# Hybrid decoder step on one core: query weights of two chunks split between GpSimd's and SP's transfers

## What is computed

```python
q = (xc @ w_q).reshape(PEER_BLOCK, PEER_HEADS, 2, PEER_DK)
s = jnp.einsum('chsk,hsnk->chsn', q, sub_keys).astype(jnp.float32)
sv, si = lax.top_k(s, PEER_TOPK)
cand = sv[:, :, 0, :, None] + sv[:, :, 1, None, :]
...
cs, sel = lax.top_k(cand.reshape(PEER_BLOCK, PEER_HEADS, PEER_TOPK * PEER_TOPK), PEER_TOPK)
...
u = u_tab[eidx]
act = jax.nn.gelu(jnp.einsum('chkd,cd->chk', u, xc).astype(jnp.float32))
w = (g * act).astype(xc.dtype)
return jnp.einsum('chk,chkd->cd', w, v_tab[eidx])
```

## Time and profile before

| | |
|---|---|
| median of 3 runs | 3100.81 us (3096.8 to 3101.7) |
| profiled execution, its own time | 3100.0 us |
| its span | 3097.7 us |
| TensorE matmul busy | 2381.0 us (77%) |
| VectorE busy | 2150.3 us (69%) |
| ScalarE busy | 1003.2 us (32%) |
| GpSimd busy | 1220.6 us (39%) |
| moved | 1229.46 MB, mean 397 GB/s |
| of it by GpSimd's queue | 1082.20 MB, 84.4% of 16 engines' span |

### The profile page before, as it was taken

One profiled execution on the slowest core, in us unless ns is written; L12 is line 12 of the kernel. 1 busy time (PEld: TensorE's weight loads), 2 busy tenths in 40 slices (PEclk: granted clock), 3 DMA queues, 4 the chain that ended last, 5 costly groups with the idle time before them and its releaser, 6 DMA issues.

```text
span 3097.7 us, 40697 instructions
## 1 busy us (share of the span) xinstructions
PE 2381.0 (77%) x14548; PEld 1198.2 (39%) x14548; DVE 2150.3 (69%) x5355; ACT 1003.2 (32%) x3276; POOL 1220.6 (39%) x1048
## 2 busy tenths in 40 slices
PE   8997768898877778898877768888877675655565
PEld 7764324555343334455334324454433331111111
DVE  7757887765479886665468987666558887554445
ACT  2224433422334332432234332432133433222223
POOL 0014443334344443433343444344344445444443
PEclk9998889999988989989978879899998887677778
DMA  4549999999999999999999999999999999999997
GB/s 150 203 195 419 420 421 421 416 420 418 412 421 416 421 421 418 419 392 420 421 413 421 420 421 418 407 393 420 418 420 421 420 419 417 419 403 421 421 420 324
DMA packets 178185, 1229.46 MB, mean 397 GB/s; under 512 B 22696, under 2 KB 23080, under 8 KB 31936
## 3 DMA queue, kind: packets, MB, share of 16 engines
q0 software_dynamic: 148608, 1082.20, 84.4%
q1 hardware_dynamic: 27728, 139.82, 11.4%
q10 hardware_dynamic: 1648, 4.85, 0.4%
HBM read 1222.24 MB, written 4.55 MB: 396 GB/s over the span
## 4 chain that ended last, share of the span: by engine, by line
DMA 48%; PE 29%; DVE 14%; ACT 4%; issue 2%; ACTq 1%; POOL 1%; DVEq 0%; SPq 0%
DMA arena<-in_uv,arena 47%; PE psum L2032 12%; PE psum L1929 8%; DVE arena L1619 7%; ACT arena L794 3%; PE psum L2078 3%; PE psum L2092 3%; DVE arena L1190 2%; DVE arena L1198 1%; POOL arena L750 1%; PE psum L2104 1%; PE psum L1944 1%; PE psum L1968 1%; DMA arena<-in_w_ab 1%; ACTq L818 1%
## 5 line engine op out<-in xcount | busy, mean ns | idle before, releaser
L750 POOL DMA_INDIRECT arena<-in_uv,arena x1032 | 1217.4, 1180 | 1849.5 <-PE psum L2032 1494.1
L1619 DVE CUSTOM_DVE_ANT_0 arena<-arena 128x1024 f32<-128x1024 f32 x1024 | 1247.4, 1225 | 809.6 <-DMA arena<-in_uv,arena 766.4
L2032 PE MATMUL psum<-arena 64*64 64x512 f32 x8184 | 1231.4, 727 | 663.2 <-ACT arena L794 607.5
L794 ACT ACTIVATE arena<-arena 128x1 f32<-128x1 f32 (+6 forms) x2745 | 726.6, 302 | 1898.3 <-DVE arena L1619 1745.8
L2032 PEld LDWEIGHTS psum<-arena 64*64 64x64 f32 x8184 | 305.4, 152 | 1394.6 <-ACT arena L794 899.6
L1929 PE MATMUL psum<-arena 128*128 128x256 f32 (+1 forms) x2656 | 642.0, 397 | 7.1 <-ACT arena L794 4.4
L1929 PEld LDWEIGHTS psum<-arena 128*128 128x128 f32 x2656 | 510.4, 197 | 198.6 <-issue 124.9
L1190 DVE TENSOR_TENSOR arena<-arena 128x512 f32<-128x512 f32 (+12 forms) x559 | 249.6, 473 | 11.8 <-issue 0.4
L794 ACT ACT_TABLE_LOAD x121 | 155.2, 1283 | 4.1 <-PEq L2380 0.8
L794 ACT ACTIVATE arena<-psum 128x256 f32<-128x256 f32 (+5 forms) x254 | 98.7, 403 | 148.6 <-PE psum L1929 109.7
L2078 PE MATMUL psum<-arena 128*128 128x128 f32 (+2 forms) x640 | 120.2, 345 | 6.7 <-DMA arena<-in_w_ab 5.8
(11 more groups left out here) (112 smaller groups left out, 966.6 us busy)
## 6 DMA issues: line engine op xcount, KB each, us to landing
arena<-in_w_in SPq DMA_DIRECT2D x56, 1024.0 KB
arena<-in_w_q SPq DMA_DIRECT2D x34, 1024.0 KB
arena<-in_uv,arena POOLq DMA_INDIRECT x1032
arena<-in_w_ab SPq DMA_DIRECT2D x12, 1024.0 KB
arena<-in_w_out SPq DMA_DIRECT2D x11, 512.0 KB, 17.0
arena<-in_keys SPq DMA_DIRECT2D x17, 256.0 KB, 8.2
arena<-in_w_ab SPq DMA_DIRECT2D x8, 512.0 KB, 10.4
arena<-in_x_tok SPq DMA_DIRECT2D x8, 512.0 KB
```

The costliest lines, as they stand in the source:

```text
L750: pool.indirect_dma_start(uvring[:, r], None, i_["uv"], bass.IndirectOffsetOnAxis(column, 0)).then_inc(uv_in[r], 16)
L794: return nc.scalar.activation(out, in_, f, **kw)
L1619: V.tensor_tensor_reduce(out=u, in0=u, in1=hn[i // (SLOT // 2)], scale=1.0, scalar=0.0, op0=ALU.mult, op1=ALU.add, accum_out=dots_[:, b % ...
L2032: ins = mm(PV[o:o + HP, half], dg[r:r + HP, PAIR * (b % 2) + k], uvring[r:r + HP, place(c, i) % UV, at:at + 512], start=(i % (SLOT // 2) = ...
```

## The change

The query weights of chunks 1 and 2 (the second and third; `SHARED`), 16 pairs, come in two transfers each. Rows 0 to 119 are issued by GpSimd (`query_weights`) just before one particular gather (`gather_before` works out which: one whose slot TensorE frees in a batch that stands, in its order, behind the last projection that used the weights' slot). Rows 120 to 127 stay with SP, at the place in its queue where the whole load was. Both issuers wait on the same value of `unit`. TensorE waits for both semaphores. The first and the last chunk, and all other weights, stay as they are.

```diff
+WIDE = 120
+SHARED = [(c, 48 + 2 * h) for c in (1, 2) for h in range(HEADS)]
+SHARED_AT = {ring_at(c, l): (c, l) for c, l in SHARED}
...
+def wide_loads(g):
+
+    return sum(k <= g and k % RING == g % RING for k in SHARED_AT)
...
+def spent_units(c, l):
+
+    at = PAIRS[c].index(pair_of(c, l)) - RING
+    before = c if at >= 0 else c - 1
+    return units(before) + slot_unit(before, PAIRS[before][at][-1]) + 1
...
+def gather_before(c, h):
+
+    t = AT_PROJ + 6 * (h - 1) - 2
+    b = own(c - 1) + steps_at(c, t)
+    at = PAIR * (b + 1) + UV + 2
+    return (c, at - SLOT) if at >= SLOT else (c - 1, at)
+
+
+POOL_LOADS = {gather_before(c, (l - 48) // 2): (c, l) for c, l in SHARED}
...
-                        sp.dma_start(ring[:, g % RING, 0:size], flat(w)[:, at:at + size]).then_inc(slot_in[g % RING], 16)
+                        rows = slice(WIDE, P) if g in SHARED_AT else slice(0, P)
+                        sp.dma_start(ring[rows, g % RING, 0:size], flat(w)[rows, at:at + size]).then_inc(slot_in[g % RING], 16)
...
+            def query_weights(c, l):
+
+                pool.wait_ge(unit, spent_units(c, l))
+                name, m = weight(c, l)
+                g, w = ring_at(c, l), flat(i_[name][m // 2])
+                pool.dma_start(ring[0:WIDE, g % RING, 0:w.shape[1]], w[0:WIDE]).then_inc(wide_in[g % RING], 16)
+
             def gathers(c, first, last):
 
                 for i in range(first, last):
+                    if (c, i) in POOL_LOADS:
+                        query_weights(*POOL_LOADS[c, i])
...
                 pe.wait_ge(slot_in[g % RING], 16 * (g // RING + 1))
+                if g in SHARED_AT:
+                    pe.wait_ge(wide_in[g % RING], 16 * wide_loads(g))
```

More of the change, by code:

```diff
@@ L522, in build @@
         nf_ok, fin_ok = sem("nf_ok"), sem("fin_ok")
+        wide_in = [sem(f"wide_in{k}") for k in range(RING)]
         slot_in = [sem(f"slot_in{k}") for k in range(RING)]
@@ L631, in slot_free @@
                 if home(c, l) is None and l == pair_of(c, l)[0]:
-                    at = PAIRS[c].index(pair_of(c, l)) - RING
-                    before = c if at >= 0 else c - 1
-                    sp.wait_ge(unit, units(before) + slot_unit(before, PAIRS[before][at][-1]) + 1)
+                    sp.wait_ge(unit, spent_units(c, l))
             for g2 in range(2):
```

## The result

The changed kernel takes 3215.73 us (3214.31 to 3218.58) against 3100.47 us: ratio 1.0377, 95% interval 1.0364 to 1.0389. It is 115.3 us slower, where 5.0 were forecast and the range ended at 3113. The profiled execution's span is 3216.5 us.

A forecast was written before the change was run, and what follows sets the result against it. It took full DMA engines at 421 GB/s to bound the kernel. Its six terms, 0 + 5.0 + 0 + 0 + 0 + 0, gave +5.0 us, 3105.8 us against the median, with a range of 3088 to 3113.

The forecast's parts named there:

- What bounds the kernel: Whole ring of nine slots: DMA engines full at 421 GB/s from 800 us on; only 25.5 us of idling recoverable.
- Point 1, bytes: The 16 split loads: not a byte is added or removed, so 0 us by volume.
- Point 2, the spread: Rows per DMA engine in the 16 split loads: some engines get a ninth row, 0.311 us each, +5.0 us.
- upper bound of +39.8 us: Worst case for the spread over engines: all 8 rows on an engine with eight already, 16 x 8 x 0.311.
- Points 3 to 5: SP's queue unchanged, GpSimd's 16 added issues covered by DMA work, its added wait already met: 0 us each.
- Point 6, late weights: Query weights behind GpSimd's gathers, issued 22 to 47 us later, still land in time for TensorE: 0 us.
- The relieved engine: Rival: the engine left out by the 120 rows is the one behind; 3089.8, or 3080 at best; chance 0.25.
- Late weights: Rival: TensorE waits for query weights at the second chunk's first three heads, 15.5 us in all; 3121.3; chance 0.09.
- All 8 rows on one engine: Rival: SP's eight rows all go to one full engine in each load, +39.8 us, 3141; chance 0.03.
- The rotating deal: Rival: the engine left out changes from load to load, 8 rows net each, +2.5 us, 3103.3; chance 0.08.
- What would show it: Signs: query phases 2.5 us longer each; wrong if span below 3094 or TensorE waits over 5 us for weights.

## Why the prediction was wrong

- **What bounds the kernel: right.** DMA engines full, TensorE and VectorE with room. It is why what was lost in the two phases came out at the end: 114.0 of 115.3.
- **Point 1, bytes: right in itself**, 1229.46 MB before and after, and of no use: the rate changed, not the volume.
- **Point 2, the spread: this is the step that failed.** It said that "a row of 8192 bytes takes 0.311 us" on whichever engine it lies, and then counted rows. The deal itself was as assumed, as far as the increments show: fifteen engines with eight rows. But 0.311 us is the price in full transfers and gathers. Where a load is cut by rows, its own rows and the rows of the gathers beside it take longer, and the sum had no term for that. The 120 rows, which it had at 0, cost 100.7 us; the eight, which it had at 5.0, cost 14.6. That the rows meet in SBUF is Theory A's account, argued and not shown. The upper bound of +39.8 us was taken from the same count and so was no bound. The sign of a missing term stood in the prediction: it quoted the rule of the Trainium skill (DMA: Bandwidth & Descriptors, "Rules for kernel authors") that two transfers to parts of the partitions do not gain, read it as "engines that are full whoever issues", and gave it no price. The earlier trace rows hold no weight load cut by rows, so they could not agree with a rule on parts. The runs bear the rule out and go beyond it: the cut does not only gain nothing, it costs 3.8 us a load as halves from SP.
- **Points 3 to 5: right.** SP's queue kept its place, GpSimd's issues took 0.56 us where 0.94 was put, and the run with all 128 rows from GpSimd shows that issue and wait together cost nothing (3098.59).
- **Point 6, late weights: nearly right, and by luck.** 0 was taken; TensorE waited 3.8 us, under the 5 us named as a sign. But the loads take 26 us to land in the second chunk and not 14 to 18. The second and third land at 888.38 and 925.77 us, 13 and 21 us after TensorE wanted them before (875.58 and 904.92); that it waited 1.5 us for each is because the slower gathers had held it up as well.
- **The relieved engine: half right.** There is a late engine; the one left out is another. **Late weights:** 3.8 us, not the 15.5 of the rival. **All 8 rows on one engine:** no, eight engines report one row each. **The rotating deal:** the increments name no engine, so whether it is the same one each time is open; at a price of 2.5 us it explains nothing here.
- **What would show it:** I named the phases' length and a span below 3094, and nothing for a share that stays at 1 while the rate falls. That pair would have named the fault in the first row.

## What to carry to other kernels

When DMA engines are full, cut a load by columns and not by partitions: here a cut by rows cost 3.8 to 7.5 us per load of 1 MiB, a cut by columns nothing. Read the DMA share and the rate together; a full share with a low rate meant here that transfers held each other up, and moving the cut load to SP's queue took away a third of the cost, not all. And a price per row taken from full transfers holds for full transfers only.

## What I had not expected of the hardware

- A load of 1 MiB as eight transfers of 16 neighbouring partitions each cost 7.4 us more than one full transfer; with every eighth partition in each, 4.1; as two halves of 64 rows, 3.8. In the first case 93 us of the sixteen loads' cost were longer packets of the gathers beside them.
- The same cut costs 1.7 to 1.8 times as much in GpSimd's queue (101.7 against 60.1, 100.7 against 55.2) while an uncut load costs the same in both (3098.59 against 3099.08).
- Eight rows of 8 KB to partitions 120 to 127 cost 0.91 us per transfer beside GpSimd's 120 rows, 1.3 us beside SP's; by volume they are 0.16 (64 KB at 421 GB/s).
- One part of each gather read is late: in the kernel before it comes 8.07 us behind the first one at 2897.52 us, where the other fifteen lie within 2.57.
- TensorE's waits for these weights stand in the list of waits with 0.7 us; the increments of the semaphores show 3.8.
